# Two-layer block stack on one core: RWKV solves on quarter matrices, a reordered layer close and a folded Hyena transform

## The reference

```python
def second_block(x, p, ...):
    for i in range(DEPTH):                       # DEPTH = 2
        mix = even_mixer(h, ...) if i % 2 == 0 else odd_mixer(h, ...)
        h = layer_norm(DEEPNORM_ALPHA * h + mix @ w_out[i], ln_g[i], ln_b[i])
        e = rms_norm(p[i] @ ple_w[i], ple_norm[i])
        h = h + jax.nn.sigmoid(h @ ple_gate[i]) * e

# even_mixer: a gated delta rule (4 heads of 128) and an RWKV-7 scan (8 heads of 64), both directions
# odd_mixer:
    x1, x2, v = jnp.split(dwconv_centred(xv, conv_w, conv_b), 3, axis=-1)
    filt = hyena_filters(...)                    # circ / (sum(abs(circ)) + eps)
    z = x1 * (fft_long_conv(v, filt[:, 0]) + skip[0] * v)
    y = x2 * (fft_long_conv(z, filt[:, 1]) + skip[1] * z)
    return y * jax.nn.silu(gate)

def fft_long_conv(u, filt):                      # seq = 256, transforms of 512
    return jnp.fft.irfft(jnp.fft.rfft(u, n=2 * seq, axis=1) * jnp.fft.rfft(filt, axis=0)[None], n=2 * seq, axis=1)[:, :seq]
```

## Time and profile before

| | |
|---|---|
| runs, median | 2069.02 us |
| profiled execution, its own time | 2072.83 us |
| its span, first to last instruction | 2071.5 us |
| mean granted TensorE clock, share of 2.4 GHz | 0.872 |
| PE busy, DVE busy, ACT busy, POOL busy | 1685.7, 1178.3, 741.0, 87.1 us |

### The profile page before, as it was taken

The page is one execution under the profiler, slowest core; times in us unless marked ns, Lnnn a source line. Parts: engine busy times, 40 slices in busy tenths (PEclk is TensorE's granted clock), DMA queues, the critical chain, the costliest instruction groups (busy, mean ns, idle before and its releaser), DMA issues.

```text
span 2071.5 us, 24051 instructions
## 1 busy us (share of the span) xinstructions
PE 1685.7 (81%) x10132; PEld 1472.1 (71%) x10132; DVE 1178.3 (57%) x1913; ACT 741.0 (36%) x1145; POOL 87.1 (4%) x70
## 2 busy tenths in 40 slices
PE   2978997999797899799996958644997779877867
PEld 1968886998696898589886857534987558833445
DVE  2456556555545755555557656358765558546555
ACT  2444444444344443344445412122211434422133
POOL 0000010000000001000000010000000000002300
PEclk8989998999898999899997979656876889968879
DMA  5543334555453333445563301000001434520022
GB/s 168 163 140 102 102 123 142 163 184 183 145 179 124 102 116 109 142 158 185 186 206 101 102 23 40 0 0 0 1 1 44 153 114 144 171 62 10 0 76 102
DMA packets 151176, 220.97 MB, mean 107 GB/s; under 512 B 6228, under 2 KB 110684, under 8 KB 150428
## 3 DMA queue, kind: packets, MB, share of 16 engines
q1 hardware_dynamic: 151068, 219.43, 33.2%
HBM read 218.35 MB, written 1.06 MB: 106 GB/s over the span
## 4 chain that ended last, share of the span: by engine, by line
PE 68%; DVE 19%; ACT 6%; DMA 4%; issue 2%; POOL 1%; SPq 1%; DVEq 0%; ACTq 0%
PE bank L368 16%; PE bank L370 15%; PE bank L369 15%; PE bank L1656 4%; DVE weights_low L344 3%; PE bank L1736 2%; PE bank L772 2%; PE bank L2745 2%; PE bank L2766 2%; PE bank L1886 2%; ACT weights_high L333 1%; PE bank L1713 1%; DVE place L2067 1%; PE bank L2721 1%; PE bank L1864 1%
## 5 line engine op out<-in xcount | busy, mean ns | idle before, releaser
L344 DVE TENSOR_TENSOR weights_low<-place,weights_high 128x1024 fp32r<-128x1024 f32 (+2 forms) x387 | 446.5, 1196 | 225.4 <-ACT weights_high L333 225.1
L333 ACT ACTIVATE weights_high<-place 128x1024 fp32r<-128x1024 f32 (+2 forms) x387 | 378.2, 1029 | 165.6 <-DMA place<-w_in_dram 66.6
L368 PE MATMUL bank<-hT_high,weights_high 128*128 128x256 f32 x1152 | 336.4, 292 | 3.6 <-ACT hT_high L449 1.4
L370 PE MATMUL bank<-hT_high,weights_low 128*128 128x256 f32 x1152 | 329.4, 286 | 0.0
L369 PE MATMUL bank<-hT_low,weights_high 128*128 128x256 f32 x1152 | 328.9, 286 | 0.0
L368 PEld LDWEIGHTS bank<-hT_high,weights_high 128*128 128x128 f32 x1152 | 222.2, 193 | 9.5 <-DVE hT_low L459 2.1
L369 PEld LDWEIGHTS bank<-hT_low,weights_high 128*128 128x128 f32 x1152 | 221.9, 193 | 0.7
L370 PEld LDWEIGHTS bank<-hT_high,weights_low 128*128 128x128 f32 x1152 | 221.4, 192 | 0.0
L1656 PE MATMUL bank<-place,place 128*128 128x128 f32 x624 | 86.9, 303 | 48.8 <-DVE place L2015 22.6
L1656 PEld LDWEIGHTS bank<-place,place 128*128 128x128 f32 x624 | 82.8, 214 | 54.0 <-issue 43.2
L370 PE MATMUL bank<-weights_high,branchT_low 128*128 128x512 f32 x256 | 101.0, 395 | 0.0
(11 more groups left out here) (403 smaller groups left out, 3504.0 us busy)
## 6 DMA issues: line engine op xcount, KB each, us to landing
place<-w_in_dram SPq DMA_DIRECT2D x48, 1024.0 KB, 5.2
place<-w_up_dram SPq DMA_DIRECT2D x32, 1024.0 KB, 5.5
place<-w_down_dram SPq DMA_DIRECT2D x32, 1024.0 KB, 4.9
place<-even_w_in_dram SPq DMA_DIRECT2D x17, 1024.0 KB, 5.3
place<-w_out_dram SPq DMA_DIRECT2D x16, 1024.0 KB, 5.1
place<-odd_w_in_dram SPq DMA_DIRECT2D x16, 1024.0 KB, 5.4
place<-w_branch_dram SPq DMA_DIRECT2D x12, 1024.0 KB, 5.1
place<-ple_gate_dram SPq DMA_DIRECT2D x8, 1024.0 KB, 5.1
```

What stands on the lines that cost most here:

```text
L333: nc.scalar.activation(high[:, lo:hi], self.raw[p % SLOTS][:, lo:hi], ACT.Copy).then_inc(*A("high", p, j))
L344: nc.vector.tensor_tensor(low[:, lo:hi], self.raw[p % SLOTS][:, lo:hi], high[:, lo:hi].bitcast(FP32), ALU.subtract).then_inc(*V())
L368: nc.tensor.matmul(out, left[0], right[0], start=first, stop=False)
L370: return nc.tensor.matmul(out, left[1], right[0], start=False, stop=last)
```

## The change

1. **Solves.** The second step takes only the 64x64 quarter between the two 64-blocks, the third only the quarter of the second block. The first step stays whole. ACT and DVE copy out 64 partitions in place of 128.
2. **Close, both layers.** `w_out_2` comes ahead of `ple_w` in the pieces, `pT` ahead of the rows. PE turns `mixed` and multiplies by `w_out_2` first; the `ple_w` product stands behind the first transposes of `x`, and the second transposes stand in the middle of the first tile's `ple_gate` products. ACT's copies of the `ple` banks and DVE's scaling of `e` go to the end.
3. **Hyena, arithmetic.** The second half of the tokens is held in reverse order (`reverse` table, an f32 matmul in place of a transpose). Sum and difference of the halves (`folded`) are then transformed by one 128x128 matrix for each tile: signal 4 matmuls in place of 8 for each half of the channels, inverse 4 in place of 8. The norm is multiplied into x1 and x2, the skip is added to the real spectrum tiles by four further 128-column matmuls each. GpSimd does nothing any more.
4. **Hyena, order.** The channels of v are projected first. Filters, sums, norm and the first spectrum of order 0 are spread over the later `pair` iterations; the rest is interleaved with the two `silu` halves. Two pieces of the ring are left blank.

```diff
@@ solve_tensor
-    for j, (mats, right, wait) in enumerate(((v.XT, rhs, ready), (v.masked, U, [("solved", *tag, 0)]), (v.XT, work, [("solved", *tag, 1)]))):
+    steps = ((v.XT, rhs, whole, whole, ready), (v.masked, U, first, then, [("solved", *tag, 0)]),
+             (v.XT, work, then, then, [("solved", *tag, 1)]))
+    for j, (mats, right, rows, out, wait) in enumerate(steps):
...
-            ins = nc.tensor.matmul(b[:, i * width:(i + 1) * width], mats[:, u, :], right[:, i, :], start=True, stop=True)
+            ins = nc.tensor.matmul(b[out, i * width:(i + 1) * width], mats[rows, u, out], right[rows, i, :], start=True, stop=True)
@@ close_tensor
+    k.turn_tensor(("mixedT", i), c.mixed, KT, mixed_ready, reverse=reverse)
+    for t in range(TT):
+        k.token_tile(("w_out_2", i), w_out, t, c.hT, WB, k.turned("mixedT", i))
+    k.turn_tensor(("xT", i), c.x, KT, ready, 0)
     for half in range(2):
         k.token_major(("ple", i, half), [(("ple_w", i, half), 2)], c.pT, WB, lambda t, kk: [("pT_cut", i)])
...
+    k.token_tile(("ple_gate", i), ple_gate, 0, c.hT, WB, gated, [0])
+    k.turn_tensor(("xT", i), c.x, KT, ready, 1)
+    k.token_tile(("ple_gate", i), ple_gate, 0, c.hT, WB, gated, [1])
+    k.token_tile(("ple_gate", i), ple_gate, 1, c.hT, WB, gated)
@@ odd_tensor
+    k.T.wait_ge(("odd_tables_loaded",))
...
+        if n in (4, 5):
+            filter_tensor(k, o, 0, 0, n - 4)
+        elif n in (6, 7):
+            filter_tensor(k, o, 0, 1, n - 6)
+        elif n == 8:
+            sums_tensor(k, o, 0, 0)
+        elif n == 9:
+            norm_tensor(k, o, 0, 0)
+        elif n == 10:
+            spectrum_tensor(k, o, 0, 0)
+    k.token_major(("silu", "hy", 0), k.halves_of(("silu", "hy", 0)), o.hT, WB, h_ready)
+    conv_turned_tensor(k, o, *HY_PIECES[-1])
+    sums_tensor(k, o, 0, 1)
+    for hf in range(2):
+        signal_tensor(k, o, 0, hf)
+    norm_tensor(k, o, 0, 1)
+    spectrum_tensor(k, o, 0, 1)
+    for hf in range(2):
+        for f in range(2):
+            filter_tensor(k, o, 1, hf, f)
         if hf == 0:
...
+            k.token_major(("silu", "hy", 1), k.halves_of(("silu", "hy", 1)), o.hT, WB, h_ready)
+            inverse_tensor(k, o, 0, 0)
+    inverse_tensor(k, o, 0, 1)
+    for hf in range(2):
+        sums_tensor(k, o, 1, hf)
+    for hf in range(2):
+        signal_tensor(k, o, 1, hf)
+        norm_tensor(k, o, 1, hf)
+    for hf in range(2):
+        spectrum_tensor(k, o, 1, hf)
+    for hf in range(2):
+        inverse_tensor(k, o, 1, hf)
@@ spectrum_tensor, new
+        if real:
+            for j in range(4):
+                ins = nc.tensor.matmul(b[:, j * P:(j + 1) * P], o.skips[:, 4 * hf + j:4 * hf + j + 1].to_broadcast([P, P]),
+                                       k.table("ident"), start=False, stop=j == 3)
@@ odd_vector, behind the 12 projections
+    mag_vector(k, o, 0, 1)
+    for _ in range(2):
+        k.low_of_next()
+    for hf in range(2):
+        fold_vector(k, o, 0, hf)
+    sums_vector(k, o, 0, 1)
+    differ_vector(k, o, 0, 1)
+    weigh_by_norm_vector(k, o, 0, 1)
+    for f in range(2):
+        filter_vector(k, o, 1, 0, f)
+    product_vector(k, o, 0, 0)
+    mag_vector(k, o, 1, 0)
+    for f in range(2):
+        filter_vector(k, o, 1, 1, f)
+    gate_tokens_vector(k, o, 0, 0)
+    product_vector(k, o, 0, 1)
...
@@ close_pieces behind the silu pieces of the odd layer
+    k.blank()
+    k.blank()
     close_pieces(k, 1)
+    for half in range(2):
+        k.hold(("w_out_2", 1, 1, half), *[("inverse", HY_ORDER - 1, 1, which) for which in "AB"])
```

More of the change, by code:

```diff
@@ new lines, in signal_tensor, with inverse_tensor @@
+def signal_tensor(k, o, n, hf):
+    nc, T = k.nc, k.T
+    left = split(k.table("dft_signal"), 4, P)
+    for tile, part in enumerate((0, 1, 1, 0)):
+        b = k.claim("signal", n, hf, tile)
+        T.wait_ge(("folded", n, hf))
+        nc.tensor.matmul(b, left[:, tile, :], o.folded[:, hf, part, :], start=True, stop=True).then_inc(*T("signal", n, hf, tile))
+def inverse_tensor(k, o, n, hf):
+    nc, T = k.nc, k.T
+    left = split(k.table("idft"), 4, P)
+    for which, tiles in (("A", (0, 3)), ("B", (1, 2))):
+        b = k.claim("inverse", n, hf, which)
+        T.wait_ge(("product", n, hf))
+        for j, tile in enumerate(tiles):
+            ins = nc.tensor.matmul(b, left[:, tile, :], o.H[n][:, hf, tile, :], start=j == 0, stop=j == 1)
+        ins.then_inc(*T("inverse", n, hf, which))
@@ new lines, in differ_vector, with weigh_by_norm_vector @@
+def differ_vector(k, o, n, hf):
+    nc, V, mag, cut = k.nc, k.V, o.mag[n][hf], HALVES[hf]
+    V.wait_ge(("sums", n, hf))
+    nc.vector.tensor_tensor(mag[:, 0], o.ft[:, 0, :, cut], o.ft[:, 1, :, cut], ALU.add).then_inc(*V())
+    nc.vector.tensor_tensor(mag[:, 1], o.ft[:, 0, :, cut], o.ft[:, 1, :, cut], ALU.subtract).then_inc(*V("differed", n, hf))
+def weigh_by_norm_vector(k, o, n, hf):
+    nc, V = k.nc, k.V
+    V.wait_ge(("norm", n, hf))
+    for t in range(TT):
+        s = o.xv[:, n, t, HALVES[hf]]
+        nc.vector.tensor_tensor(s, s, k.bank("norm", n, hf), ALU.mult).then_inc(*V())
+    V.same("free", "norm", n, hf)
@@ new lines, in odd_scalar @@
+    for half in range(2):
+        k.high_of_next()
+    spectrum_scalar(k, o, 0, 0)
+    mag_scalar(k, o, 0, 1)
+    for t in range(TT):
+        A.wait_ge(("silu", "hy", 0, t))
+        nc.scalar.activation(o.mixed[:, t, HALVES[0]], k.bank("silu", "hy", 0, t), ACT.Silu).then_inc(*A("free", "silu", "hy", 0, t))
+    conv_turned_scalar(k, o, *HY_PIECES[-1])
+    deltas_scalar(k, o, 1)
+    for hf in range(2):
+        signal_scalar(k, o, 0, hf)
+    for f in range(2):
+        decay_of_filter_scalar(k, o, 1, 0, f)
@@ new lines, in odd_scalar @@
+    spectrum_scalar(k, o, 0, 1)
+    for f in range(2):
+        decay_of_filter_scalar(k, o, 1, 1, f)
+    mag_scalar(k, o, 1, 0)
+    for t in range(TT):
+        A.wait_ge(("silu", "hy", 1, t))
+        nc.scalar.activation(o.mixed[:, t, HALVES[1]], k.bank("silu", "hy", 1, t), ACT.Silu).then_inc(*A("free", "silu", "hy", 1, t))
+    inverse_scalar(k, o, 0, 0)
+    mag_scalar(k, o, 1, 1)
+    inverse_scalar(k, o, 0, 1)
+    k.high_up_to(("w_out_2", 1, 0, 1))
+    for hf in range(2):
+        signal_scalar(k, o, 1, hf)
@@ L2929, in filter_scalar @@
-    for hf, cut in enumerate(HALVES):
-        A.wait_ge(("norm", n, hf))
-        nc.scalar.activation(o.norm[:, cut], k.bank("norm", n, hf), ACT.Copy).then_inc(*A("free", "norm", n, hf))
-def spectrum_scalar(k, o, n):
-    nc, A = k.nc, k.A
-    for hf, cut in enumerate(HALVES):
-        for tile in range(4):
-            A.wait_ge(("signal", n, hf, tile), ("spectrum", n, hf, 4))
-            nc.scalar.activation(o.U[:, tile, cut], k.bank("signal", n, hf, tile), ACT.Copy).then_inc(*A("free", "signal", n, hf, tile))
```

599 lines of the change are left out of this document (320 added, 279 removed).

## The result

| | before | changed |
|---|---|---|
| runs, median (lowest to highest) | 2069.35 us (2068.97 to 2074.03, 4 runs) | 1996.7 us (1987.65 to 1998.81, 4 runs) |
| profiled execution, its span | 2071.5 us | 1986.1 us |
| granted clock over the span | 0.872 | 0.890 |

The ratio is 0.9637, 95% interval 0.9609 to 0.9665. The forecast of 1990.5 us lies 6 us under the median, inside its range.

A forecast was written before the change was run, and what follows sets the result against it. PE was taken to have work queued but not always weights, banks or clock. Savings of 10 (solves), 15.5 (close 0), 39 (odd layer) and 14 (close 1) sum to 78.5 us, giving 1990.5 us, range 1963 to 2018.

The forecast's parts named there:

- I take 10: RWKV solves: 10 us saved over the eight later steps, from a worked range of 7 to 14; bounds -14 and +3.
- Odd layer to the last projection: Hyena layer's start up to the last projection: 113 us after the change, 87.3 before, because work is added there.
- The tables' wait (a): Odd layer's start: PE waits for tables fetched last, and the reversed half costs two records for one; +2.7 us (0.9 to 4).
- Tail: Last projection to the mixer's end in the odd layer: 133 us after, 198 before; bounds 110 and 160.
- bank wait: Behind the last projection, PE stands 7.7 us for bank 3, which ACT copies only after cutting two pieces of weights.
- product waits: Odd layer's tail: PE waits for DVE's products, 12.7 us before an inverse of order 0 and 5.1 us at the last.
- 1 us more: Close 1: `w_out_2`'s second half, fetched after the mixer's end behind `pT` and the rows, costs 1 us more than close 0.
- PE as bound throughout: Rival, 12%: DVE's second product meets a free PE, bank and product waits vanish; odd layer 25 us less, 1965 us.
- Quarter solves bring nothing: Rival, 15%: a single quarter does not shorten the solves, or each shape change exposes a tail; 2000.5 us.
- Close gives half: Rival, 14%: weight cuts, now behind the second tile's norm, decide both closes; 2005.5 us.
- Tail at half clock: Rival, 12%: odd layer's tail stays DVE-bound, PE gets 1.2 GHz for half its 96 us or more; about 2015 to 2030.
- Slower than before: Rival, 2%: the interleaved odd layer never gets 2.4 GHz from iteration 4 on; all of it at half clock gives 2150.

The follow-up runs named there:

- second profile: The changed kernel run once more, unaltered: 1996.27 us, ratio 0.9652.
- solves alone: The kernel before with only the changed solve functions (quarter solves), close and Hyena as before: 2061.12 us, ratio 0.9970.
- the form on 128: The changed kernel with RWKV's second and third solve steps contracting over all 128 rows, still loading 64 columns of weights: 1988.58 us, ratio 0.9619.
- early product: The changed kernel with DVE making the first product of order 0 before multiplying the filters of order 1: 1984.24 us, ratio 0.9599.
- Early fetch: The changed kernel with the odd layer's second half of `w_out_2` fetched after DVE's last product, ahead of `pT` and the rows: 1985.58 us, ratio 0.9606.
- close alone: The kernel before with only the reordered close in both layers, solves and Hyena as before: 2033.64 us, ratio 0.9850.

## Why the prediction was right, point by point

The changed kernel is read from its second profile, which is near its median; us saved:

| part | predicted | measured | by |
|---|---|---|---|
| solves | 10 | 6, net | ratios of the solves alone |
| close 0 | 15.5 | 13.2 | windows |
| odd layer | 39 | 41.9 | windows |
| close 1 | 14 | 10.1 | windows |
| sum | 78.5 | 71.2; 72 by the ratio 0.9652 | |

The three measured windows set one execution of before (2072.8 us, slower than its usual 2066 to 2069) against one of the changed kernel. With RWKV and the start taken in the same way (11.6 us) the sum is 76.8, the difference of the two spans. That 71.2 meets 72 therefore owes something to luck. In the forecast, too, errors partly cancel: two closes and the solves were put 2 to 4 us too high each, the odd layer 3 too low.

- **Solves.** The price of a step was right: 0.86 us less at full clock, 1.70 less at half (predicted 0.9 and 1.7), and a change of shape shows no more than 0.15 us. The eight steps gave 13.7 us, against the 7 to 14 worked out. The step that failed is "I take 10", as a net: it had no term for the clock. That moves this stretch by 6 us with unchanged code (141.5 or 135.4), and the form on 64 rows took 7 us more of it than the form on 128.
- **Close 0.** PE stood at bank 7 for 3.9 us (predicted 3), at the second half's weights for 4.1 (predicted 4). The second `ple_gate` tile starts 58 us behind the mixer's end, predicted 56: these 2 us are what is missing. The half tile behind the first stand took 7.9 us (1620.89 to 1628.80), where the prediction has 5.5 (1641.5 to 1647): its first eleven products ran at half clock. For the half behind the second stand the prediction had half clock, and 8 us; it took 8.2.
- **Odd layer to the last projection.** 111 us (1663.4 to 1774.4 in the first profile, as much in the second), predicted 113. The tables' wait (a), +2.7, did not come: PE's wait ahead of the first transposes ended with DVE (9.3, L1459). In the profile with the early product it ended with the DMA, after 9.2 us: the two are level.
- **Tail.** 132 us, predicted 133: bank wait 7.4 (7.7), product waits 12.4 (12.7) and 4.9 (5.1), GpSimd idle, DVE's product operations at 0.69 us. This was the largest term; each of the three waits that were worked out from the in-order lists came within 0.3 us. The Hyena edits were not run alone. By the runs they bring what is left, 72 less 6 for the solves and 31 less 7 for the closes (whose second fetch comes late here), 42 us; how that divides between the halved products, the idle GpSimd and the new order is not shown.
- **Close 1.** The step that failed is "1 us more" for the late fetch. The first DMA was issued at 1908.88 us, behind `pT` and three rows, and ACT could cut it 10.0 us later, not after the 5.4 of the earlier trace rows; PE stood 8.0 us. The prediction had no term for the 1.8 MB ahead of it. Early fetch and close alone both save 17 us, where the fetch is early.
- **Rivals.** PE as bound throughout: no, the two waits are in the trace, though an order of DVE's list takes the larger away. Quarter solves bring nothing: no. Close gives half: no. Tail at half clock: no, its clock was 0.90. Slower than before: no. The solves did come 4 us short, though not for the reasons that their rival names.

## What to carry to other kernels

Read an engine's in-order list for operations whose operands are ready while the engine stands for something else: moving one product brought 9.6 us of the odd layer, of which close 1 took back 2.8. What paces these small matmuls is the number of weight columns. With 64 columns, 128 rows gave the better clock here; where the data allow both forms, run both. Count the bytes that stand in the queue ahead of a fetch. Compare stretches of several profiles before giving a gain to a change: here one pair of profiles showed 19.8 us for an edit worth 6.

## What was not expected of the hardware

- The granted clock over the same RWKV instructions was 0.79 with 64-row steps and 0.85 with 128-row steps, 124.7 against 117.4 us, although a step lasts 1.14 or 1.15 us in either at full clock. In one unit of four the single step went the other way.
- Two DMAs of 1 MB, issued behind `pT` and three broadcast rows, took 11.0 us to land in the median, where four of the same size 30 us later took 5.0: the DMA engines were full, at 336 GB/s, and 1.8 MB lay ahead.
- Removing a wait of PE can go with a slower stage behind it: close 1 took 79.1, 81.9 or 82.6 us (clock 0.90, 0.86, 0.85) with the same instructions, after edits in the layer ahead of it. What decides it is not settled.
